# Weight remainders of the second feed-forward's up panels: an accumulating DMA in place of a VectorE subtraction

## What is computed

```
h = rms_norm(x, norm_mlp)
x = x + square(relu(h @ w_up)) @ w_down      # w_up: 1024 x 4096, w_down: 4096 x 1024
return rms_norm(x, norm_final)
```

## Time and profile before

| | us |
|---|---|
| median of 3 runs | 1496.56 |
| lowest and highest run | 1496.21, 1496.62 |
| span of the profiled execution, first to last instruction | 1494.7 |
| PE busy in it | 1485.1 |
| DVE busy | 876.2 |
| ACT busy | 565.4 |
| POOL busy | 24.2 |

### The profile page before, as it was taken

How to read it: one execution, slowest core, us unless ns; L and a number is a source line. 1 busy time by engine, 2 the same in 40 slices (tenths; PEclk the granted TensorE clock), 3 DMA queues, 4 the chain that set the end, 5 groups by cost and what they waited for, 6 DMA issues and landing times.

```text
span 1494.7 us, 20331 instructions
## 1 busy us (share of the span) xinstructions
PE 1485.1 (99%) x7240; PEld 1226.2 (82%) x7240; DVE 876.2 (59%) x1425; ACT 565.4 (38%) x836; POOL 24.2 (2%) x21
## 2 busy tenths in 40 slices
PE   9999999999999999999999999999999999999998
PEld 7878888888888888888888887888888888888887
DVE  6737764775665655443468877965665653255433
ACT  5215553333433333323325656444443331123231
POOL 0000000000000000000000000000000000000000
PEclk9999999999999999999999999999999999999999
DMA  6623222223322232333333223322122322333221
GB/s 234 226 87 97 77 91 85 85 83 101 112 88 95 98 98 98 99 102 110 113 99 106 94 97 102 110 76 84 61 81 85 109 91 96 98 99 98 99 71 57
DMA packets 44445, 149.17 MB, mean 100 GB/s; under 512 B 4792, under 2 KB 7352, under 8 KB 44260
## 3 DMA queue, kind: packets, MB, share of 16 engines
q1 hardware_dynamic: 39840, 138.43, 28.3%
q10 hardware_dynamic: 4548, 9.96, 1.9%
HBM read 146.24 MB, written 6.06 MB: 102 GB/s over the span
## 4 chain that ended last, share of the span: by engine, by line
PE 98%; issue 0%; DMA 0%; DVE 0%; ACT 0%; SPq 0%; POOLq 0%; POOL 0%; DVEq 0%; ACTq 0%
PE ps L1168 31%; PE ps L1170 31%; PE ps L1169 31%; PE ps L1319 1%; PE ps L1332 1%; PE ps L2340 1%; PE ps L1209 0%; DMA x<-x_dram 0%; PE ps L1202 0%; PE ps L2360 0%; PE ps L1377 0%; PE ps L2372 0%; PE ps L2440 0%; PE ps L2285 0%; PE ps L1274 0%
## 5 line engine op out<-in xcount | busy, mean ns | idle before, releaser
L528 ACT ACTIVATE wh<-stage 128x1024 fp32r<-128x1024 f32 x254 | 268.9, 1059 | 544.3 <-PE ps L1170 540.0
L1168 PE MATMUL ps<-hh,wh 128*128 128x512 f32 x1088 | 430.7, 396 | 0.3 <-DVE wl L764 0.3
L1170 PE MATMUL ps<-hh,wl 128*128 128x512 f32 x1088 | 424.3, 390 | 0.0
L1169 PE MATMUL ps<-hl,wh 128*128 128x512 f32 x1088 | 423.6, 389 | 0.0
L764 DVE TENSOR_TENSOR wl<-stage,wh 128x1024 fp32r<-128x1024 f32 x253 | 309.3, 1223 | 185.2 <-ACT wh L528 184.7
L1168 PEld LDWEIGHTS ps<-hh,wh 128*128 128x128 f32 x1088 | 204.3, 188 | 46.7 <-issue 3.9
L1170 PEld LDWEIGHTS ps<-hh,wl 128*128 128x128 f32 x1088 | 204.2, 188 | 43.5
L1169 PEld LDWEIGHTS ps<-hl,wh 128*128 128x128 f32 x1088 | 204.5, 188 | 39.8
L1168 PE MATMUL ps<-ah,wh 128*128 128x512 f32 (+1 forms) x448 | 171.7, 383 | 0.0
L1170 PE MATMUL ps<-ah,wl 128*128 128x512 f32 (+1 forms) x448 | 171.5, 383 | 0.0
L1169 PE MATMUL ps<-al,wh 128*128 128x512 f32 (+1 forms) x448 | 171.5, 383 | 0.0
(11 more groups left out here) (340 smaller groups left out, 1839.3 us busy)
## 6 DMA issues: line engine op xcount, KB each, us to landing
stage<-stream_dram SPq DMA_DIRECT2D x254, 512.0 KB, 3.3
bias_lines<-bias_line ACTq DMA_DIRECT2D x1, 3840.0 KB
bias<-bias_lines ACTq DMA_DIRECT2D x4, 512.0 KB, 4.8
x<-x_dram SPq DMA_DIRECT2D x3, 512.0 KB, 7.3
out_dram<-x SPq DMA_DIRECT2D x12, 128.0 KB, 1.9
bias<-bias_lines ACTq DMA_DIRECT2D x4, 256.0 KB, 2.9
mem<-mem_dram ACTq DMA_DIRECT2D x1, 1024.0 KB, 4.8
stage<-stream_dram SPq DMA_DIRECT2D x2, 256.0 KB, 4.0
```

Of the source, the lines that this page charges most:

```text
L528: A(parts_of(b, p)[0], b.stage[:, p.slot, :], ACT.Copy).then_inc(s.hi_ready, 1)
L1168: MM(out, wh, xh, start=start, stop=False, skip_group_check=True)
L1169: MM(out, wh, xl, start=False, stop=False, skip_group_check=True)
L1170: return MM(out, wl, xh, start=False, stop=stop, skip_group_check=True)
```

## The change

For the 32 up panels of the second feed-forward (`rest_by_dma`), the remainder `wl` is made in another way. ACT runs a second copy behind `hi`, with scale -1, from `stage` into `wl`: the rounding gives the negated hi part. POOL then issues a DMA that reads `stage` and adds it onto `wl`, within SBUF: `wl = -hi + stage`. POOL takes these transfers one at a time (`rest`): it waits for ACT's copy and for `lo_ready` of all panels before, issues the transfer, waits until it has landed (`rest_in`), and counts `lo_ready` up. DVE's `lo` returns at once for these panels; at the first down panel of each half it gains a wait on `lo_ready`, so that the count stays in order. On POOL the first four transfers stand between `power(4)` and `power(5)`, the other 28 behind `power(5)`. Some semaphores of the first block are shared, to free numbers for this. The core of the diff:

```diff
+def rest_by_dma(p):
+    n = p.index if isinstance(p.index, int) else p.first
+    return P_UP_A <= n < P_DOWN_A or P_UP_B <= n < P_DOWN_B
...
         A(parts_of(b, p)[0], b.stage[:, p.slot, :], ACT.Copy).then_inc(s.hi_ready, 1)
+        if rest_by_dma(p):
+            A(parts_of(b, p)[1], b.stage[:, p.slot, :], ACT.Copy, scale=-1.0).then_inc(s.negated_hi.sem, 1)
...
+        if rest_by_dma(p):
+            return
         dve.wait_ge(s.hi_ready, p.index + 1)
+        if isinstance(p.index, int) and p.index in (P_DOWN_A, P_DOWN_B):
+            dve.wait_ge(s.lo_ready, p.index)
...
-    for n in (4, 5):
-        power(n)
+    power(4)
+    def rest(p, n, i):
+        pool.wait_ge(s.negated_hi.sem, s.negated_hi.base + 16 * n + p.index - (P_UP_B if n else P_UP_A) + 1)
+        pool.wait_ge(s.lo_ready, p.index)
+        G.dma_start(f32(b.wl[:, p.slot, :]), b.stage[:, p.slot, :], accum_op=ALU.add).then_inc(s.rest_in, 16)
+        pool.wait_ge(s.rest_in, 16 * (p.index - (P_UP_B - 16 if n else P_UP_A) + 1))
+        pool.sem_inc(s.lo_ready, 1)
+    for u in range(RING):
+        rest(Panel(P_UP_A + u), 0, 0)
+    power(5)
+    for n, first in enumerate((P_UP_A, P_UP_B)):
+        for i in range(0 if n else 1, FH // 4):
+            for u in range(RING):
+                rest(Panel(first + u + RING * i), n, i)
```

More of the change, by code:

```diff
@@ L140, with __init__ @@
     pass
+class Counted:
+    def __init__(self, sem, base):
+        self.sem, self.base = sem, base
 def semaphores(nc):
@@ L161, in semaphores @@
         "rs_ready row_done row_ready u_ready")
-    (s.va_gelu, s.ln_mean, s.ln_pow, s.v_normed) = named(
-        "va_gelu ln_mean ln_pow v_normed")
+    (s.va_gelu, s.dots_mean, s.ln_pow, s.v_normed) = named(
+        "va_gelu_negated_hi dots_mean ln_pow v_normed")
     (s.ws_masked, s.spatial_done, s.pooled, s.poolmm_done) = named(
         "ws_masked spatial_done pooled poolmm_done")
-    (s.lam_dots, s.lam_exps, s.v_done, s.qk_hi) = named(
-        "lam_dots lam_exps v_done qk_hi")
+    (s.lam_exps, s.v_done, s.qk_hi) = named(
+        "lam_exps v_done qk_hi")
     (s.qk_ready, s.v_hi, s.v_ready, s.bias_in) = named(
@@ L228, in semaphores @@
     s.x_in = named(" ".join(f"x_in{n}" for n in range(4)))
+    s.negated_hi = Counted(s.va_gelu, 1)
+    s.rest_in = nc.alloc_semaphore("rest_in")
     return s
@@ L588, in scalar_program @@
     hi(Panel(P_POOL + 1 + RING))
-    act.wait_ge(s.lam_dots, 1)
+    act.wait_ge(s.dots_mean, 1)
     A(b.lam_e, b.lam_d, ACT.Exp).then_inc(s.lam_exps, 1)
@@ L817, in vector_program @@
     st.link(V.tensor_tensor(prod, lam[:, :, 0, :], lam[:, :, 1, :], ALU.mult))
-    V.tensor_reduce(b.lam_d, prod, AX_X, ALU.add).then_inc(s.lam_dots, 1)
+    V.tensor_reduce(b.lam_d, prod, AX_X, ALU.add).then_inc(s.dots_mean, 1)
     dve.wait_ge(s.consts_in, 16)
@@ L845, in vector_program @@
     var = b.ln_mv.rearrange("p (t c) -> p t c", c=2)
-    V.tensor_scalar(b.ln_var, var[:, :, 1], 1e-5, None, ALU.add).then_inc(s.ln_mean, 1)
+    V.tensor_scalar(b.ln_var, var[:, :, 1], 1e-5, None, ALU.add).then_inc(s.dots_mean, 1)
     evac_row(Panel(P_POOL + 1), E_POOL + 1, b.xb[:, 1, 16:], 1)
@@ L1130, in gpsimd_program @@
     power(1)
-    pool.wait_ge(s.ln_mean, 1)
+    pool.wait_ge(s.dots_mean, 2)
     G.tensor_tensor(b.ln_rs, b.ln_var, b.expo[:, 0:4], ALU.pow).then_inc(s.ln_pow, 1)
```

## The result

The changed kernel takes 1503.86 us (median of 4 runs, 1503.15 to 1504.16) against 1496.46 us for the kernel before beside it (4 runs, 1496.21 to 1496.62). The ratio is 1.0048 with a 95% interval of 1.0036 to 1.006: slower by about half a per cent, 7.4 us. The span of its profiled execution is 1502.2 us against 1494.7, 7.5 more.

The account below looks back on a forecast made before the run. PE's own work was taken as the bound, so every term added 0: the profiled span stays 1494.7 us, plus 1.9 us to the median gives 1496.6 us. The range was 1494.5 to 1538 us.

Parts of the forecast that it names:

- The likeliest case, no wait: In both up halves PE never waits for the transfers; time within 0.2% of before, 1495 to 1499 us, chance 0.52.
- rival (a): Reload and accumulating transfer slow each other fully, R 6.07 to 7.3; 1506 us at 6.3, 1538 at 7.3; chance 0.27.
- What bounds the kernel: In the up halves and the down half between, PE's own work is the bound; DVE, ACT and POOL have room.
- Parts 1 and 2: DVE loses 32 subtractions (39 us), ACT gains 32 copies (34 us); neither was to change the time.
- Part 3, the law: PE's wait in the up halves: 16R - 95.8 in half B; 11R - 65.1 or 16R - 96.0 in half A.
- R: Time from one POOL transfer's release to the next one's; taken as 5.65 us, range 3.2 to 7.3.
- the other term: Half A, 11 transfers from the sixth panel, held by ACT's copy: PE waits 11R - 65.1, nothing up to 5.92.
- `power(5)` in time: In half A, the power behind four transfers is in time (about 1146) up to R = 6.3; cost 0 below that.
- Part 3, the size of R: Byte counts plus 1.4 us for start and landing gave 5.0 to 6.3 us; the middle, 5.65, meant no wait.
- The add: The accumulation inside POOL's transfers: must read two tiles; no profile row showed one, so its cost was unseen.
- The estimate by that rule: One transfer alone, priced with two source reads at half a copy's rate: 2.0 + 2 x 1.2 = 4.4 us, no wait.
- Part 4: DVE's new wait at the first down panel delays work queued behind it; cost 0, with 4 us to spare.

## Why the prediction was right or wrong

The time lies in the stated range, which says little, since the range reaches up to 1538 us. The likeliest case, no wait, did not happen. The time is that of rival (a) near its lower end, which had a chance of 0.27, but what (a) says is only a part of the cause.

- **What bounds the kernel**: right. PE was full, DVE's 39 us bought nothing, and the loss is PE's waiting, at a clock of 1.00.
- **Parts 1 and 2**: right, by the run with the copies alone (ratio 1.0). Their sizes: DVE 37.8 us for 39, ACT 27.3 for 34 (copies back to back overlap in their rows).
- **Part 3, the law**: right, but for one point. Above R = 6.18 or so the prediction lets the 16 transfers in a row bind in half A, 16 x 6.25 - 96.0 = 4.0 us. In the trace the sixth transfer still waited for ACT's copy (6.56 us in POOL's timeline), so the other term held, 11 x 6.25 - 65.1 = 3.65; the half lost 3.4. With 16 x 6.22 - 95.8 = 3.72 for half B the sum is 7.4 us, as measured. The runs with half A alone, without POOL's own wait and with one more power agree within 0.2 us. `power(5)` in time: right at 6.25 (it began at 1144.61, ahead of the 1146 that the prediction allowed), and late at 7.3.
- **Part 3, the size of R**: this is the step that failed. R was 5.65 in the sum and 6.25 on the chip, on the other side of the 5.9 to 6.0 at which waiting begins. The landing itself came out near it, at 5.6, in part by luck, since 5.65 was the middle between two byte rates; the data phase was 4.5 us, inside the 3.6 to 4.9 that they gave. What the sum left out is POOL's turn-around from a landing to its next issue, 0.63 to 0.77 us in the chain; it took "landed" for "next one issued". The 1.4 us of start and landing were taken from a load that nobody waits for in single file, and there was no term for the waiting engine's own steps. The period reads as 4.5 us for a transfer without a reload beside it, 1.1 for the reload and about 0.65 for the turn-around. The loss needs all of them: without the reload the period in half A was 5.25 and without the add (1204.63 - 1152.86) / 10 = 5.18, and a landing of 5.6 with no turn-around would by the law have cost nothing.
- **The reload beside it**: rival (a) has the two slow each other fully. The transfer's landing grew by 1.1 us, by the run with short reloads, while the reload's own median in the stages of the two up halves went from 3.3 and 3.4 us to 3.5 and 3.6. With the 5.6 us that this makes, (a) alone stays below the 6.0 from which it was to decide. The Trainium skill (DMA: Bandwidth & Descriptors, section "Issuing engines are not separate DMA queues") states that DMAs of all issuers interleave on the same engines; the run with short reloads agrees, 4.5 against 5.6 us.
- **The add**: the prediction left it unseen. It moved 205 GB/s alone, against 437 in the best window of a plain load, and took 5.8% against 2.8% of the DMA engines' time with and without it. The Trainium skill (Collectives: The Full Stack, section "The bandwidth ceiling: the fold count and why AG ≠ RS ≠ AR") says that a ReduceScatter runs at about half the rate of an AllGather because its add needs two source reads. The rows here agree on the half; that the second read is the reason no run here shows. The estimate by that rule, 4.4 us for a transfer alone, stands beside a smallest landing of 4.5. But the sum by that rule, no wait, was wrong for the same reason as the other: it priced a transfer, not a period.
- **Part 4**: right. DVE stood 12.3 us at its new wait, and PE began down half A without a wait on DVE or ACT. The last `al` of half A was done at 1235.5, about 2 us before PE came to it (1226.73 + 2 x 5.44 = 1237.6), where the prediction had 4 to spare:

```profile
1221.14 1.23 DVE L786 TENSOR_TENSOR wl<-stage,wh 128x1024 fp32r<-128x1024 f32 x1 [12.34 <-POOLq L1184]
...
1234.84 0.69 DVE L2139 TENSOR_TENSOR al<-tmp,ah 128x512 fp32r<-128x512 f32 x1 [0.70 <-ACT ah L532]
```

## What to carry to other kernels

Where an engine waits for each DMA before it issues the next, compare the pitch of the work with the whole period: issue, data beside whatever the same release sets off, landing, and the waiting engine's own steps up to the next issue. A lead of several buffers hides the latency of one transfer but not, over many panels, a period above the pitch; here PE first stopped at the thirteenth of 16 panels, so the first ones look well. Two transfers in flight, each with its own semaphore, took the dead time out of the period here and brought the time back to that of before (1496.57 against 1496.37 us), which is all there was to win in a stage that PE fills.

## What was not expected of the hardware

An accumulating transfer of 512 KB within SBUF takes POOL 0.87 us to issue against 0.53 for a plain one. Beside a reload that was issued with it a plain transfer landed in 4.7 us, and ahead of the reload in 2.9. Two accumulating transfers in flight beside a load drew 187 to 189 GB/s through the DMA engines over a whole half with landings of 6.0 us, against 163 to 166 GB/s and 5.6 us in single file. The pitch of the single file was not the same from kernel to kernel (6.12 to 6.25 us) although the work in it was; why was not looked into.
